# A two-layer transformer trunk on one core: ScalarE's activation step is called one weight chunk earlier

## The reference

```python
for i in range(DEPTH):                       # DEPTH = 2
    mod = (silu(c) @ mod_w[i] + mod_b[i])[:, None, :]
    sh_m, sc_m, g_m, sh_f, sc_f, g_f = jnp.split(mod, 6, axis=-1)
    h = x * (1.0 + sc_m) + sh_m
    y = attention(h) if i % 2 == 0 else short_conv(h)      # w_qkv, w_o / w_in, w_out
    x = layer_norm(ALPHA * x + (1.0 + g_m) * y)
    h = x * (1.0 + sc_f) + sh_f
    y = square(relu(h @ w1[i] + b1[i])) @ w2[i] + b2[i]    # 2048 -> 8192 -> 2048
    x = layer_norm(ALPHA * x + (1.0 + g_f) * y)
```

## Time and profile before

| | |
|---|---|
| Median of three runs | 2261.99 us |
| The profiled execution | 2261.99 us |
| its span | 2260.3 us |
| PE busy | 2202.7 us (97%) |
| PE weight loads busy | 1847.7 us (82%) |
| DVE busy | 1735.4 us (77%) |
| ACT busy | 1131.5 us (50%) |
| DMA queue of SP, share of 16 engines | 81.9% |

### The profile page before, as it was taken

One profiled execution on the slowest core, in us unless ns is written; L12 is line 12 of the kernel. 1 busy time (PEld: TensorE's weight loads), 2 busy tenths in 40 slices (PEclk: granted clock), 3 DMA queues, 4 the chain that ended last, 5 costly groups with the idle time before them and its releaser, 6 DMA issues.

```text
span 2260.3 us, 27641 instructions
## 1 busy us (share of the span) xinstructions
PE 2202.7 (97%) x10534; PEld 1847.7 (82%) x10534; DVE 1735.4 (77%) x1790; ACT 1131.5 (50%) x1409; POOL 7.7 (0%) x25
## 2 busy tenths in 40 slices
PE   6999999999999999999999999999999999999998
PEld 5999987877888888888787887888778888888886
DVE  7899999976878777777878899877756665655666
ACT  4777784455345445435454443336443543543552
POOL 0000000000000000000000000000000000000000
PEclk9999999999999999999999999999999999999999
DMA  9999998789989989888859989976877777866772
GB/s 353 388 387 397 398 364 305 252 303 316 321 288 321 314 296 306 308 300 288 302 162 347 351 289 340 322 248 223 270 269 236 246 255 238 254 198 194 213 249 96
DMA packets 306867, 650.14 MB, mean 288 GB/s; under 512 B 22048, under 2 KB 53296, under 8 KB 304688
## 3 DMA queue, kind: packets, MB, share of 16 engines
q1 hardware_dynamic: 303776, 631.33, 81.9%
q10 hardware_dynamic: 2960, 17.05, 1.9%
HBM read 623.12 MB, written 2.10 MB: 277 GB/s over the span
## 4 chain that ended last, share of the span: by engine, by line
PE 78%; DVE 10%; DMA 5%; ACT 3%; issue 3%; SPq 1%; DVEq 0%; ACTq 0%
PE bank L1325 23%; PE bank L1326 22%; PE bank L1327 22%; DMA stage<-stage 3%; DVE w_low L961 3%; PE bank L1315 3%; PE bank L1318 3%; PE bank L1317 3%; DVE mod_acc L917 2%; DMA mod_raw<-in_mod_w 1%; SPq L530 1%; ACT stage L832 1%; DVE stage L1154 1%; ACT hid_high L839 1%; ACT stage L835 1%
## 5 line engine op out<-in xcount | busy, mean ns | idle before, releaser
L656 ACT ACTIVATE w_high<-raw 128x1024 fp32r<-128x1024 f32 x752 | 785.3, 1057 | 945.3 <-PE bank L1327 919.3
L961 DVE TENSOR_TENSOR w_low<-raw,w_high 128x1024 fp32r<-128x1024 f32 x752 | 910.5, 1221 | 335.0 <-ACT w_high L656 334.2
L1325 PE MATMUL bank<-w_high,h_high 128*128 128x512 f32 x1632 | 641.3, 393 | 19.1 <-DVE w_low L961 19.1
L1327 PE MATMUL bank<-w_high,h_low 128*128 128x512 f32 x1632 | 637.5, 391 | 0.0
L1326 PE MATMUL bank<-w_low,h_high 128*128 128x512 f32 x1632 | 637.5, 391 | 0.0
L917 DVE SCALAR_TENSOR_TENSOR mod_acc<-mod_raw,cond,mod_acc 128x1024 f32<-128x1024 f32 x345 | 441.8, 1280 | 31.9 <-DMA mod_raw<-in_mod_w 27.7
L1325 PE MATMUL bank<-w_high,hid_high 128*128 128x512 f32 x1120 | 437.2, 390 | 6.7 <-DVE hid_low L1161 4.7
L1326 PE MATMUL bank<-w_low,hid_high 128*128 128x512 f32 x1120 | 435.9, 389 | 0.0
L1327 PE MATMUL bank<-w_high,hid_low 128*128 128x512 f32 x1120 | 435.9, 389 | 0.0
L1325 PEld LDWEIGHTS bank<-w_high,h_high 128*128 128x128 f32 x1632 | 307.7, 189 | 89.8 <-DVE w_low L961 22.3
L1327 PEld LDWEIGHTS bank<-w_high,h_low 128*128 128x128 f32 x1632 | 307.6, 189 | 65.1
(11 more groups left out here) (145 smaller groups left out, 1094.0 us busy)
## 6 DMA issues: line engine op xcount, KB each, us to landing
raw<-in_mlp_w SPq DMA_DIRECT2D x512, 512.0 KB, 4.8
mod_raw<-in_mod_w SPq DMA_DIRECT2D x368, 512.0 KB, 7.3
raw<-in_attn_w_qkv SPq DMA_DIRECT2D x96, 512.0 KB, 10.6
raw<-in_conv_w_in SPq DMA_DIRECT2D x96, 512.0 KB, 5.5
stage<-stage SPq DMA_DIRECT2D x176, 128.0 KB, 3.2
raw<-in_attn_w_o SPq DMA_DIRECT2D x32, 512.0 KB, 8.0
raw<-in_conv_w_out SPq DMA_DIRECT2D x32, 512.0 KB, 5.5
mod_raw<-in_mod_w SPq DMA_DIRECT2D x32, 256.0 KB, 6.5
```

The lines of the kernel that those rows point to most:

```text
L656: act.activation(chunk_slots(n)[0], raw[:, n % NCH], ACT.Copy).then_inc(high_done, 1)
L961: dve.tensor_tensor(low_, raw[:, n % NCH], high.bitcast(F32), ALU.subtract).then_inc(raw_used, 1)
L1325: pe.matmul(dst, high[:, k, c], wh, start=first, stop=False, skip_group_check=True)
L1327: return pe.matmul(dst, low[:, k, c], wh, start=False, stop=last, skip_group_check=True)
```

## The change

`late()` is called behind `high` of chunk 5 of a group, where it was called behind `high` of chunk 6.

```diff
@@ def highs(w, late=None, first=SLOTS):
                 for j in range(first, NCH):
                     high(w * NCH + j)
-                    if late and j == SLOTS + 2:
+                    if late and j == SLOTS + 1:
                         late()
                 for j in range(SLOTS):
                     high((w + 1) * NCH + j)
```

## The result

The changed kernel takes 2335.74 us (median of four, 2332.59 to 2339.29) against 2261.84 for the kernel before, measured beside it: 1.0327 times as long, 95% interval 1.0309 to 1.0346. It is slower by 74 us; the forecast was 58 in a range of 30 to 83. Its profiled execution has a span of 2336.8, which is 76.5 more.

The account below looks back on a forecast made before the run. PE, busy 97% of the span, was taken to bound the kernel. Waits by part summed to 53 us (8 + 7 + 9 + 11 + 11 + 3 + 4), the clock added 5: 2262 + 58 = 2320, range 2292 to 2345.

Parts of the forecast that it names:

- The late step already waits for its swap: ACT's late step waits 53.6 us for swap DMAs, in 23 of 32 cases, so calling it earlier starts it no earlier.
- One group's own shift: Group worked in layer 0, block 1: `low` 7 comes 3.3 us later (2.1 plus 1.2 for a tile); PE waits about 1.0.
- The loop through the transposes: DVE's chain from one transposes' start to the next grows from 20.7 to 23.4 us, over PE's 21.76, so delay builds up.
- the sign that the prediction named: Transposes should start later behind E, PE's end of the previous group, within a block; staying near E + 3 refutes the loop.
- The other parts: Waits outside layer 0's blocks 1 and 2: block 3 at 9, blocks 0 at 11 each, layer 1's rest 3, convolution 4.
- The two blocks 0: First MLP block of each layer: residual passes crowd DVE, the shift costs in full, 8 to 13 us a block, 11 taken.
- Layer 1's later blocks: Layer 1, blocks 1 to 3: loop of 20.6 us, under PE's 21.76, nothing builds up; 1 to 6 us, 3 taken.
- The clock: Lower granted clock behind new PE waits, six at 1.6 us: 10 at most, nothing at least, 5 us taken.
- Shift without loop: Rival, chance 0.20: DVE catches up between late steps, each group pays only its own shift: 39 us, 2301.
- faster: Rival, chance 0.04: late step and `hid_low` come a chunk earlier, PE gets back some 5 us: 2252.
- The loop at its densest: Rival, chance 0.20: tiles stand together at the steps that count, and clock drops follow: 83 us, 2345; middle of case 2338.
- The DMA page: Rule: issue a DMA early, wait late; the change does the reverse. Its 2.3 us estimate for a swap would give 2310.

Follow-up runs that it names:

- e2: The changed kernel with DVE's mod tile additions from the first MLP group on made on 8 of 1024 columns: 2307.42 us.
- e8: The kernel before with ACT's late step one chunk later, behind chunk 7 instead of chunk 6: 2270.96 us, 1.0053 of the kernel before.
- e10: The changed kernel with mod tile loads from the first MLP group on cut from 1024 to 64 columns, DVE's work whole: 2305.80 us.

## Why the prediction held, point by point

- *The late step already waits for its swap, so it would not start earlier.* Held. In blocks 1 to 3 of layer 0 it starts at E + 8.6 to 15.3 in the kernel after, against 9.3 to 14.8. Where it had not waited before (9 of the 32) it gains at most 0.7.
- *One group's own shift, 2.1 plus a tile.* Held to a tenth in the group that was worked (22.8 against 21.8).
- *The loop through the transposes.* Half held. The delay does pass from group to group. By the sign that the prediction named, the loop failed: the transposes should start later behind E from group to group, and they start at E + 3.6, 5.0, 2.9, 4.7 in block 1. That was a poor sign, since PE waits as well and E moves with the delay. From one start of the transposes to the next block 1 took 24.1, 23.7 and 26.6 us, where the forecast had 23.4 and 25.1 at its densest, and PE's idle time grew by 8.7 and 9.1 in blocks 1 and 2, where 8 and 7 were taken. What the step left out is the second road, the landing of the swaps. The trace's 6.84 from transposes to late step was carried through unchanged, and it became up to 11.2 (group at 911.5, where the kernel before had 8.4). So the loop at 19.7 us without tiles should have lost nothing in these blocks, and e2 lost 15.3.
- *The other parts.* Their sum came out by some luck: 48.9 of waits where 53 were forecast, from terms that are off both ways. The two blocks 0 have 16.2 against 22 and block 3 has 5.1 against 9. Layer 1's later blocks have 6.3 against 3; of their delay of 8.9, some 6 arise in the three groups whose late steps start at E + 11 and more (E = 2012.5, 2213.2 and 2236.2).
- *The clock.* This is the term that was mis-sized: 5 taken, 10 named as its most, 23.8 measured, and that is more than the whole miss (74 against 58). The mean granted clock shows it too, 0.985 against 0.996 over the whole span: 0.015 x 2336.8 - 0.004 x 2260.3 = 26. I priced the waits singly at 1.6 and counted six. In the traces the clock is low in 4 stretches of the kernel before between 60 us and the last block's end, and in 15 of the kernel after. Eleven of these last 3.4 us and cost 1.7 each, near my price; four last 6.8 and cost 3.4 each. So eleven new stretches came where six were counted, and four of the fifteen cost double.
- *The rivals.* "Shift without loop" (2301) and "faster" are out. "The loop at its densest" (2338) came out nearest in size, but by the clock (23.8, where it had 10) and not by denser tiles: its waits sum to 73, and 49 were measured.
- *The DMA page.* The Trainium skill (DMA: Bandwidth & Descriptors, "Rules for kernel authors") has the rule to wait late. e8, the kernel before and the changed kernel take 2271, 2262 and 2336 for late 7, 6 and 5: waiting earlier is what costs most, but waiting later than the data's other users allow costs too. By the Trainium skill's "Anatomy of one DMA" on the same page, which fits DMAs issued from GpSimd, such a swap takes an estimated 2.3. These swaps, issued from SP beside the loads, took 2.5 at the shortest, 3.3 at the median and 7.8 at the longest.

## What to carry to other kernels

Before a waiting step is moved ahead on an in-order engine, look whether it already waits where it is: if so, it will start no sooner, and what it is moved past is late by the rest of the wait and by the step itself (for `high` 6, 2.2 and 3.8 us in the group worked in the prediction). To make such a step early, make its data early; here DVE's transposes one step sooner, with the swaps one load sooner, gave 1%, with the step left where it was. And move the consumer on the other engine along, or its old order keeps the result from those who wait for it.

## What the runs showed of the hardware that was not expected

- Four swap DMAs of 128 KB inside SBUF landed in 3.0 us (median) in one group and in 6.0, at most 7.8, two groups on, behind eight loads of 512 KB issued within 9.6 us. With the mod loads cut to 32 KB (e10) the median of blocks 1 to 3 of layer 0 was 3.1 and the longest 5.2.
- In the kernels before and after, the granted clock was at its lower level for 3.4 or for 6.8 us around most PE waits of 2.0 to 5.7 us; two in the kernel before, of 2.03 and 2.33, had none. Over the kernel the new waits of 48.6 us brought 23.8 of clock, so a wait cost about half as much again as its length. The longer wait does not always have the longer stretch: in the kernel after, one of 4.16 at 960.1 had 3.4 us of lower clock, one of 3.34 at 1435.6 had 6.8.
